# First mixer's output projection: six of eight row blocks as three single-pass products, with the low weights written by GpSimd into the weight ring

## The reference, cut to what matters

```python
def even_mixer(xn, w_in, ..., w_out):
    proj = xn @ w_in
    lru_x, lru_g, rw = jnp.split(proj, [LRU_WIDTH, 2 * LRU_WIDTH], axis=-1)
    h = rg_lru(causal_dwconv(lru_x, conv_w, conv_b), ...)
    y_lru = jax.nn.gelu(lru_g) * h
    y_rwkv = rwkv7_mixer(rw, ...)     # ends: on = (o - mean) * rsqrt(var + eps) * gn_w + gn_b
                                      #       return (on + bonus) * g
    y = jnp.concatenate([y_lru, y_rwkv.astype(y_lru.dtype)], axis=-1)
    return y @ w_out                  # [256, 1024] @ [1024, 1024]
...
x = x + even_mixer(h, ...)
h = rms_norm(x, e_ln_ffn[j])
x = x + swiglu(h, e_ffn_gate[j], e_ffn_up[j], e_ffn_down[j])
```

## Time and profile before

| | |
|---|---|
| median of 3 runs | 2560.86 us (2559.83 to 2564.26) |
| span of the profiled execution, first to last instruction | 2558.8 us |
| TensorE busy, over the span | 2494.1 us (97%) |
| VectorE / ScalarE / GpSimd busy | 1928.3 / 1498.8 / 130.6 us |
| mean granted TensorE clock | 0.996 of full speed |

### The profile page before, as it was taken

One profiled execution on the slowest core, in us unless ns is written; L12 is line 12 of the kernel. 1 busy time (PEld: TensorE's weight loads), 2 busy tenths in 40 slices (PEclk: granted clock), 3 DMA queues, 4 the chain that ended last, 5 costly groups with the idle time before them and its releaser, 6 DMA issues.

```text
span 2558.8 us, 41983 instructions
## 1 busy us (share of the span) xinstructions
PE 2494.1 (97%) x15961; PEld 2113.0 (83%) x15961; DVE 1928.3 (75%) x2674; ACT 1498.8 (59%) x2177; POOL 130.6 (5%) x108
## 2 busy tenths in 40 slices
PE   8899999989999999999999999999999999999998
PEld 7676999857888888888888888857999999876998
DVE  7856556758999999999999997876655655678655
ACT  5613435457888888888788886392444443257432
POOL 0100000007301010100001000000000000010000
PEclk9999999999999999999999999999999999999999
DMA  6646453677999999999999995202554552231551
GB/s 262 247 196 253 186 186 117 236 324 293 381 360 377 356 377 360 365 369 368 368 366 365 369 358 204 115 2 115 207 181 166 197 190 106 99 132 75 222 188 50
DMA packets 90972, 619.83 MB, mean 242 GB/s; under 512 B 10208, under 2 KB 10464, under 8 KB 40800
## 3 DMA queue, kind: packets, MB, share of 16 engines
q1 hardware_dynamic: 88992, 609.17, 62.3%
q0 software_dynamic: 1280, 4.72, 0.5%
q10 hardware_dynamic: 576, 4.19, 0.5%
HBM read 615.95 MB, written 2.10 MB: 242 GB/s over the span
## 4 chain that ended last, share of the span: by engine, by line
PE 87%; DVE 7%; ACT 3%; DMA 2%; issue 1%; DVEq 0%; SPq 0%; ACTq 0%
PE psum L2032 8%; PE psum L2034 8%; PE psum L2033 8%; PE psum L436 7%; PE psum L438 7%; PE psum L437 7%; PE psum L2069 4%; PE psum L2067 4%; PE psum L2068 4%; PE psum L451 3%; PE psum L452 3%; PE psum L453 3%; DMA ring<-stream_dram 2%; PE psum L1515 1%; PE psum L2041 1%; PE psum L2591 1%
## 5 line engine op out<-in xcount | busy, mean ns | idle before, releaser
L2402 DVE TENSOR_TENSOR r_high<-ring,r_high 128x1024 fp32r<-128x1024 f32 x670 | 798.8, 1230 | 56.0 <-ACT r_high L2285 42.8
L2285 ACT ACTIVATE r_high<-ring 128x1024 fp32r<-128x1024 f32 x672 | 703.4, 1062 | 76.6 <-PE psum L2034 53.1
L436 PE MATMUL psum<-r_low,r_high 128*128 128x256 f32 x1408 | 399.7, 284 | 2.9 <-DVE r_high L526 1.4
L438 PE MATMUL psum<-r_low,r_high 128*128 128x256 f32 x1408 | 398.4, 283 | 0.0
L2032 PE MATMUL psum<-r_high 128*128 128x512 f32 x896 | 359.6, 401 | 2.0 <-DVE r_high L2393 2.0
L2034 PE MATMUL psum<-r_high 128*128 128x512 f32 x896 | 350.2, 391 | 0.0
L2033 PE MATMUL psum<-r_high 128*128 128x512 f32 x896 | 350.1, 391 | 0.0
L526 DVE TENSOR_TENSOR r_high<-ring,r_high 128x1024 fp32r<-128x1024 f32 x263 | 305.9, 1218 | 9.8 <-ACT r_high L485 9.6
L437 PE MATMUL psum<-r_high 128*128 128x256 f32 x1056 | 298.8, 283 | 0.0
L499 ACT ACTIVATE arena<-psum 128x256 f32<-128x256 f32 x88 | 33.8, 384 | 435.7 <-PE psum L438 432.9
L436 PEld LDWEIGHTS psum<-r_low,r_high 128*128 128x128 f32 x1408 | 269.9, 192 | 8.9 <-DVE r_high L3174 2.0
(11 more groups left out here) (645 smaller groups left out, 4523.9 us busy)
## 6 DMA issues: line engine op xcount, KB each, us to landing
ring<-stream_dram SPq DMA_DIRECT2D x160, 1536.0 KB, 6.5
ring<-stream_dram SPq DMA_DIRECT2D x224, 1024.0 KB, 6.8
ring<-stream_dram SPq DMA_DIRECT2D x224, 512.0 KB, 6.2
arena<-bias_dram ACTq DMA_DIRECT2D x2, 1024.0 KB, 7.8
pack<-pack_dram SPq DMA_DIRECT2D x1, 1664.0 KB, 17.0
const<-const_dram SPq DMA_DIRECT2D x1, 1060.0 KB, 13.5
x<-x_dram SPq DMA_DIRECT2D x1, 1024.0 KB, 4.9
xc<-ctx_dram ACTq DMA_DIRECT2D x1, 1024.0 KB, 7.5
```

The costliest lines, as they stand in the source:

```text
L436: pe.matmul(dst, hi, f["x_hi"][:, k, :], start=(k == 0), stop=False)
L438: ins = pe.matmul(dst, lo, f["x_hi"][:, k, :], start=False, stop=(k == KD - 1))
L2285: act.activation(dst, src, ACT.Copy).then_inc(sem("moe_w_hi"), 1)
L2402: ins = eng.tensor_tensor(lo, src, hi.bitcast(f32), SUB)
```

## The change

Blocks k = 0 and 1 stay plain float32 products. For k = 2 to 7 each product becomes three fp32r products (`EO_PLAIN = 2`). Who makes their operands:

- ScalarE copies the high weights of the six blocks into free places of the arena (`eo_hi_act`, 128x1024 each), the high part of y for blocks 2 and 3 in one instruction, and that for 4, 5 and 6, 7 in two more after `mix_fm`.
- GpSimd makes the low part of y for blocks 2 and 3 and the six low weight blocks, which it writes over the weights in the ring (`eo_low_pool`).
- VectorE makes the low parts of y for blocks 4, 5 and 6, 7 after L1552, ahead of the context's squares.
- TensorE waits, at the first part of each block, for the block's low weights (`piece_lo`), and at blocks 4 and 6 for the low parts of y (`seq_ev`), after the same wait for `mix_fm` as before.

```diff
@@ rwkv_out_pe, part(k, j)
-                if j == 0 and k % 3 == 0:
+                tk = slice(j * P, (j + 1) * P)
+                if j == 0 and k < EO_PLAIN and k % 3 == 0:
                     slot_ready(pe, n)
+                if j == 0 and k >= EO_PLAIN:
+                    pe.wait_ge(sem("piece_lo"), EO_PIECE0 + k)
+                    if k in EO_MIX:
+                        pe.wait_ge(sem("seq_ev"), 5 + EO_MIX.index(k))
                 for hf in range(2):
-                    o = (k % 3) * D + hf * 512
-                    ins = pe.matmul(psum[:, 2 + 2 * j + hf, :], yT[:, k, j * P:(j + 1) * P], slot_of[n % RING][:, o:o + 512],
-                                    start=(k == 0), stop=(k == KD - 1))
+                    cols, dst = slice(hf * 512, hf * 512 + 512), psum[:, 2 + 2 * j + hf, :]
+                    if k < EO_PLAIN:
+                        ins = pe.matmul(dst, yT[:, k, tk], eo_weights(slot_of, k)[:, cols], start=(k == 0), stop=False)
+                    else:
+                        pe.matmul(dst, eo_xh(k)[:, tk], eo_hi(k)[:, cols], start=False, stop=False)
+                        pe.matmul(dst, eo_xh(k)[:, tk], eo_weights(r_slot, k)[:, cols], start=False, stop=False)
+                        ins = pe.matmul(dst, eo_xl(k)[:, tk], eo_hi(k)[:, cols], start=False, stop=(k == KD - 1))
@@ new functions
+        EO_PLAIN, EO_MIX = 2, (4, 6)
+        def eo_hi_act(act, k0, k1):
+            for k in range(k0, k1):
+                if k == EO_PLAIN or k % 3 == 0:
+                    slot_ready(act, n_eo + k // 3)
+                act.activation(eo_hi(k), eo_weights(slot_of, k), ACT.Copy).then_inc(sem("piece_hi"), 1)
...
+        def eo_low_pool(pool):
+
+            pool.wait_ge(sem("piece_hi"), EO_PIECE0 + 1)
+            pool.tensor_tensor(eo_xl(2, 2), eo_rows(2), eo_xh(2, 2).bitcast(f32), SUB).then_inc(sem("piece_lo"), 1)
+            for k in range(EO_PLAIN, KD):
+                pool.wait_ge(sem("piece_hi"), EO_PIECE0 + k)
+                pool.tensor_tensor(eo_weights(r_slot, k), eo_weights(slot_of, k), eo_hi(k).bitcast(f32), SUB)\
+                    .then_inc(sem("piece_lo"), 1)
@@ rwkv_out_dve, behind the step that raises mix_fm
+            for i, k in enumerate(EO_MIX):
+                dve.wait_ge(sem("rw_act"), RW_STD + 1 + i)
+                dve.tensor_tensor(eo_xl(k, 2), eo_rows(k), eo_xh(k, 2).bitcast(f32), SUB).then_inc(sem("seq_ev"), 1)
             ctx_squares_dve(dve)
@@ rwkv_out_act
         def rwkv_out_act(act):
+            act.wait_ge(sem("seq_ev"), 4)
+            act.activation(eo_xh(2, 2), eo_rows(2), ACT.Copy).then_inc(sem("piece_hi"), 1)
+            eo_hi_act(act, EO_PLAIN, 3)
             act.wait_ge(sem("rw_dve"), RW_VAR)
             act.activation(t2[:, 0, :], t2[:, 0, :], ACT.Sqrt).then_inc(sem("rw_act"), 1)
+            eo_hi_act(act, 3, KD)
+            act.wait_ge(sem("mix_fm"), 1)
+            for k in EO_MIX:
+                act.activation(eo_xh(k, 2), eo_rows(k), ACT.Copy).then_inc(sem("rw_act"), 1)
@@ GpSimd's program
             lru_gelu_pool(pool)
+            eo_low_pool(pool)
             first_weights_pool(pool)
```

More of the change, by code:

```diff
@@ L883, in program @@
         N_HOMES = len(E_HOMES)
-        E_PIECES = 2 + len(E_STEPS)
+        EO_PIECE0 = 2 + len(E_STEPS)
+        E_PIECES = EO_PIECE0 + 7
         ex_hi = parts(0, 2048, "p (k t) -> p k t", k=KD)
@@ L1534, in rwkv_out_pe, with eo_weights, eo_hi, eo_xh @@
                 part(k, j)
+        EO_PLAIN, EO_MIX = 2, (4, 6)
+        n_eo = FIRST["e_out"]
+        r_slot = [r_ring[:, r * SLOT:(r + 1) * SLOT] for r in range(RING)]
+        def eo_weights(slots, k):
+            return slots[(n_eo + k // 3) % RING][:, (k % 3) * D:(k % 3) * D + D]
+        def eo_hi(k):
+            return parts((19544, 20568, 21592, 22616, 13312, 14336)[k - EO_PLAIN], D, "p (m n) -> p (m n)", m=1)
+        def eo_xh(k, n=1):
+            return parts(4096 + T * (k - EO_PLAIN), n * T, "p (m t) -> p (m t)", m=n)
+        def eo_xl(k, n=1):
+            return parts(O_YT + T * k, n * T, "p (m t) -> p (m t)", m=n)
+        def eo_hi_act(act, k0, k1):
[3 more added lines that the diff above has]
+                act.activation(eo_hi(k), eo_weights(slot_of, k), ACT.Copy).then_inc(sem("piece_hi"), 1)
+        def eo_rows(k):
+            return yT[:, k:k + 2, :].rearrange("p c t -> p (c t)")
+        def eo_low_pool(pool):
[5 more added lines that the diff above has]
+                    .then_inc(sem("piece_lo"), 1)
         def rwkv_out_dve(dve):
@@ L2914, in program @@
         n_out = FIRST["l0_out"]
-        r_slot = [r_ring[:, r * SLOT:(r + 1) * SLOT] for r in range(RING)]
         MIX_AT = (25600, 26112, 26624, 27136, 6144, 6656, 7680, 8192)
```

## The result

| | before | changed |
|---|---|---|
| median of 14 runs | 2560.22 us | 2564.33 us |
| lowest and highest | 2557.49 to 2565.31 | 2560.43 to 2567.89 |
| span of the profiled execution | 2558.8 | 2560.4 |

The ratio is 1.0016 with a 95% interval of 1.001 to 1.0023: 4.1 us slower, clear of noise but inside the 0.2% (5.1 us) that I had set as the bound for "no change". The number (2562.9, range 2557 to 2566) held. The case that I had called the likeliest did not: what happened on VectorE is rival 4, which I had given 0.08.

The account below looks back on a forecast made before the run. TensorE, holding 87% of the time, was taken as the bound. A 4.4 us stall less 4.2 saved gave +0.2, with 1.8 for the clock +2.0; on a median of 2560.86 that made 2562.9 us, range 2557 to 2566.

Parts of the forecast that it names:

- rival 4: VectorE's four gain-and-offset steps (L1550) also take turns with GpSimd; sum 4.8 us, time 2565.7; chance 0.08.
- The saving: TensorE's projection: 24 products, each as three fp32r products at 0.2276 us instead of 0.86, gain 4.2 us.
- The operands: ScalarE makes high blocks one each microsecond, GpSimd low blocks at about 2.43 us; table load hidden, 1.2 us in hand.
- The turns: VectorE steps with two SBUF inputs alternate with GpSimd's subtractions; VectorE pays 2.19 us for each of GpSimd's.
- case 5: Likeliest: VectorE's bonus and gate (L1551, L1552) take turns with GpSimd; +0.2 to +3.7 us, 2561 to 2564.6; chance 0.5.
- The size of rival 4: VectorE's chain ends near 205.9, 2.8 us later than in the likeliest case; sum 4.8 us with the clock's 1.8.
- The sign for rival 1: In the changed profile, VectorE's bonus and gate (L1595, L1596) keeping 1.2 us would show no turns there.
- The clock: After TensorE's stall ahead of block 4, half clock for 3.4 us of work; loss taken as 1.8 us, bounds 0 to 3.5.
- The FFN slot: First FFN slot there at about 219, delaying ScalarE's square; no cost, cover about 0.5 us, otherwise 1 us at most.
- Rivals 1 and 2: VectorE's chain: 1, no turns on last two steps, -4.0 us, chance 0.12; 2, VectorE keeps its turn, -2.0 us, chance 0.14.

Follow-up runs that it names:

- split kernels: Changed kernel, GpSimd making low weights of blocks 2 to 4, VectorE 5 to 7: ratio to before 0.9988; with GpSimd also waiting for VectorE's square, 0.9984.

## Why the prediction was right in its number and wrong in its case

- **The number** held in part by luck. TensorE's block 4 waits for the end of VectorE's chain, and that waits for GpSimd's last block whether bonus and gate take the turns or the gain steps do, so the wrong case cost nearly the same. And what I had added up for the right one, rival 4, was too much (below).
- **The saving** was 4.2 us by the sum. Start to start is 0.233 in this stage (22 steps from 195.46 to 200.59), not 0.2276, so a triple takes 0.70 and 24 of them save 3.9. The split kernels, without a stall, kept 3.7 of it; the last 0.2 are small gaps ahead of block 4 and of L818. Mis-sized by 0.5 us. (The record of the first fp32r product, at 194.82, is 0.64 ahead of the next. That is no extra cost: the last float32 record starts only 0.03 us before it and has its own 0.43 still to run.)
- **The operands** came as stated: high parts, table load, blocks at 2.4 us each. The table load was hidden.
- **The turns**: the mechanism was right, the place was not. The failed step is "A step of 128x256 takes 0.29 where it runs faster, so L1550 seems to run in the plain mode". The two kinds differ in more than the rate: L1550 reads two pointer scalars. The step from PSUM has the same scalars and takes 0.54, beside which 0.41 is the fast one, and rival 4, not case 5, is what happened: three gain steps of 2.3 to 2.5 us. I had also read the Trainium skill, page "SBUF — State Buffer", section "Who interferes with whom" (a tensor_scalar takes the shared pair in a two-port mode), as speaking against rival 4; with the mode read rightly it speaks for it, and the 2.3 to 2.5 us agree.
- **The size of rival 4** was added up wrongly. To case 5's stall of 4.4 I added the 2.8 us by which the chain ends later, 7.2 in all. But 1.3 of the 4.4 were the low part's wait for block 7 (203.9 to 205.2), and by the same paragraph no block was left behind this chain. Put right, the stall is 5.9 and the sum 5.9 - 4.2 + 1.8 = 3.5. Measured: a stall of 5.9, 6.1 from start to start; a clock loss of 2.6 with all small gaps in it; a saving of 3.9. That is the 4.8 of the stage, against 4.1 and 5.1 in the two medians.
- **The sign for rival 1** was badly chosen. L1595 and L1596 kept 1.2 us, which I had called the mark of no turns; they kept it because GpSimd was done before they started.
- **Case 5** is what the kernel with gain and offset from PSUM does: stall 4.7 where I had 4.4, and slower than before by 3.1 us where I had 2.0.
- **The clock** fell as it did at 598, but stayed low for 5.5 us of work where I took 3.4 to 3.6. Its cost, 2.6 us at most, lay inside the bounds of 0 to 3.5.
- **The FFN slot** had a cover of 0.5 us, which was used up: it cost 0.3 behind the stage, where I had counted nothing.
- **Rivals 1 and 2** fell: every step of two SBUF inputs that was queued while GpSimd ran waited for it, and with gain and offset from PSUM VectorE lost the turn between bonus and gate.

## What to carry to other kernels

Work moved to an idle GpSimd is not free for VectorE: list VectorE's steps of the same stretch, and count as exposed each one with two SBUF inputs and each copy or tensor_scalar from SBUF to SBUF, however short. Here four steps of 0.41 us cost 6.0 us, and a copy of two columns took 2.36. Move the operands of the exposed steps to PSUM, or let GpSimd's part end before them. To tell a mode from a duration, compare steps with the same scalars and another size or source, not merely the same shape. Before comparing two profiled spans, look where each was at the lower clock.

## What the runs showed of the hardware that I had not expected

- A float32 tensor_scalar of 128x256 with two pointer scalars takes 0.41 us from SBUF and 0.54 from PSUM; without pointer scalars 0.29 and 0.42. Beside GpSimd's two-input subtractions the form from SBUF takes up to 2.5, and the one from PSUM stays.
- A copy of 128x2 from SBUF to SBUF takes 2.29 to 2.36 us when GpSimd's 128x1024 subtraction has just begun (L3909 before, and the same step in the other profiles).
- The loss is one-sided there. GpSimd's blocks take 2.40 to 2.46 beside the tensor_scalar and 2.35 to 2.37 alone, but 3.4 behind VectorE's 1.23 us square.
- In this stretch VectorE did not once keep its turn over a waiting GpSimd instruction. Elsewhere it did: in the kernel before two of its 1.22 us subtractions (L2402) start at 592.22 and 593.36, and GpSimd's 128x8 tensor_scalar L2447 beside them takes 2.43 us, against 0.31 at 591.14. What decides is not shown.
